# The second mixer's entry in another order, latents in three weight pieces, keys without zeros, and the pooling in full f32

## The reference

```python
diff = pooled - xg                      # mean of the last 2, 4, 8 or 16 rows, less x
y = jnp.einsum('bsgc,gcd->bsgd', diff, w_grp)   # 4 groups, 256 x 256
x = layer_norm(ALPHA * x + y * scale, ...)
```

```python
mod = c_act @ w_ada[l] + b_ada[l]
sh_a, sc_a, g_a, sh_f, sc_f, g_f = jnp.split(mod[:, None, :], N_MOD, axis=-1)
h = rms_norm(x, g_mix[l]) * (1.0 + sc_a) + sh_a
x = x + g_a * hybrid_mixer(h, ...)      # differential attention and latent attention
...
proj = h @ w_in                         # dq, dk, dv, q_lat (384), kv_lat (256), k_rope (64)
q = rms_norm(q_lat, g_q_lat) @ w_q_up
kv = rms_norm(kv_lat, g_kv_lat) @ w_kv_up
```

## Time and profile before

| | us |
|---|---|
| median of 3 executions | 1013.44 (1012.06 to 1014.56) |
| profiled execution | 1015.39 |
| its span in the trace | 1013.6 |
| mean granted clock of TensorE, share of full speed | 0.989 |
| TensorE busy | 980.2 |
| VectorE busy | 657.5 |
| ScalarE busy | 496.5 |
| GpSimd busy | 62.0 |

### The profile page before, as it was taken

The page is one execution under the profiler, slowest core; times in us unless marked ns, Lnnn a source line. Parts: engine busy times, 40 slices in busy tenths (PEclk is TensorE's granted clock), DMA queues, the critical chain, the costliest instruction groups (busy, mean ns, idle before and its releaser), DMA issues.

```text
span 1013.6 us, 14978 instructions
## 1 busy us (share of the span) xinstructions
PE 980.2 (97%) x6249; PEld 891.3 (88%) x6249; DVE 657.5 (65%) x759; ACT 496.5 (49%) x662; POOL 62.0 (6%) x98
## 2 busy tenths in 40 slices
PE   6999999999999999889999999999999899999996
PEld 6888888989999999788899999988998699999996
DVE  4885468658777655875796766448778674545453
ACT  4657363535654555245275545425765464343431
POOL 1000131001000002100100000002200000000000
PEclk9999999999999999999999999998999999999998
DMA  8864355636988876363298898543553247565611
GB/s 271 282 210 161 129 172 178 232 105 208 342 283 288 268 273 213 119 211 121 85 331 312 273 307 273 196 145 123 177 191 108 90 137 231 182 188 187 185 65 42
DMA packets 114527, 200.03 MB, mean 197 GB/s; under 512 B 5122, under 2 KB 85368, under 8 KB 111388
## 3 DMA queue, kind: packets, MB, share of 16 engines
q1 hardware_dynamic: 111340, 188.38, 55.8%
q0 software_dynamic: 2832, 10.16, 2.9%
q10 hardware_dynamic: 288, 0.52, 0.1%
HBM read 198.00 MB, written 1.05 MB: 196 GB/s over the span
## 4 chain that ended last, share of the span: by engine, by line
PE 82%; DVE 8%; ACT 3%; issue 2%; SPq 1%; POOL 1%; DMA 1%; DVEq 0%; POOLq 0%; ACTq 0%
PE WB L336 11%; PE WB L332 11%; PE WB L329 11%; PE YB L348 10%; PE YB L357 10%; PE YB L353 10%; PE YB L393 4%; PE WB L348 2%; PE WB L353 2%; PE WB L357 2%; ACT wh L1015 2%; DVE U L1787 2%; DVE wl L1558 2%; PE WB L655 1%; PE WB L636 1%
## 5 line engine op out<-in xcount | busy, mean ns | idle before, releaser
L1558 DVE TENSOR_TENSOR wl<-raw,wh 128x2048 fp32r<-128x2048 f32 (+2 forms) x153 | 347.9, 2281 | 190.5 <-ACT wh L1015 189.9
L1015 ACT CAST wh<-raw 128x2048 fp32r<-128x2048 f32 (+2 forms) x153 | 288.8, 1892 | 46.3 <-PE YB L357 24.7
L329 PE MATMUL WB<-XH,wh 128*128 128x256 f32 x1024 | 145.9, 285 | 0.0
L332 PE MATMUL WB<-XH,wl 128*128 128x256 f32 x1024 | 144.3, 284 | 0.0
L336 PE MATMUL WB<-XL,wh 128*128 128x256 f32 x1024 | 143.7, 283 | 0.0
L329 PEld LDWEIGHTS WB<-XH,wh 128*128 128x128 f32 x1024 | 135.1, 192 | 3.3 <-issue 0.3
L332 PEld LDWEIGHTS WB<-XH,wl 128*128 128x128 f32 x1024 | 132.7, 193 | 0.0
L336 PEld LDWEIGHTS WB<-XL,wh 128*128 128x128 f32 x1024 | 132.1, 192 | 0.0
L348 PE MATMUL YB<-wh,FHT 128*128 128x512 f32 x360 | 112.5, 394 | 0.0
L353 PE MATMUL YB<-wl,FHT 128*128 128x512 f32 x360 | 111.6, 391 | 0.0
L357 PE MATMUL YB<-wh,FLT 128*128 128x512 f32 x360 | 111.4, 391 | 0.0
(11 more groups left out here) (316 smaller groups left out, 1115.9 us busy)
## 6 DMA issues: line engine op xcount, KB each, us to landing
raw<-in_mlp_w SPq DMA_DIRECT2D x64, 1024.0 KB, 6.2
raw<-in_w_ada SPq DMA_DIRECT2D x24, 1024.0 KB, 5.1
raw<-in_mlstm_w_in SPq DMA_DIRECT2D x12, 1024.0 KB, 7.5
raw<-in_w_ffn_gate SPq DMA_DIRECT2D x11, 1024.0 KB, 5.3
raw<-in_w_ffn_up SPq DMA_DIRECT2D x11, 1024.0 KB, 5.5
raw<-in_w_ffn_down SPq DMA_DIRECT2D x11, 1024.0 KB, 5.0
raw<-in_mem_w_kv SPq DMA_DIRECT2D x8, 1024.0 KB, 5.2
raw<-in_xattn_wq SPq DMA_DIRECT2D x8, 1024.0 KB, 7.1
```

Source lines behind the costliest of these rows:

```text
L329: e.matmul(o, H[:, at(k)], xh[:, k, :], start=k == 0, stop=False)
L332: e.matmul(o, L[:, at(k)], xh[:, k, :], start=False, stop=False)
L1015: f = e.copy(w[:, 0:a * b], raw[:, 0:a * b])
L1558: f = e.tensor_tensor(L[:, 0:a * b], raw[:, 0:a * b], H[:, 0:a * b].bitcast(F32), ALU.subtract)
```

## The change

- **Pooling.** Its chunk is no longer converted. ScalarE copies the difference in f32 to `S`, TensorE multiplies it in full f32 with the scaled `raw` buffer, two products of 256 columns a group; `pool_lows` is gone, and norm 10's `scale` waits for the window products that read x. The buffer is free for its next load (the fourth query chunk of layer 1) when the last pooling product is done. All later chunks move up one slot.
- **Norms.** `Norm.first` does centre, centre, scale, scale.
- **Modulation.** All 32 products go into the second MLP, 8 behind each of `up(14)`, `down([12])`, `up(15)`, `down([13])`; one copy and two small steps put them out, behind the conversions.
- **Entry.** The latent weights are three chunks (1920, 1792, 1920 columns), the second by two DMAs. Gate rows on TensorE: the transpositions of t = 0 stand behind two of the four instead of three. VectorE scales t = 0 ahead of the last head of norm 12, and forms the low parts between the centring and scaling of t = 1. ScalarE squares first, converts the last latent chunk, and copies gate rows between norm quarters and squares. Latents go out in the order kl 0, ql 0, kl 1, ql 1 on all engines, with kl in the banks that ql had, and their squares go to a place of their own.
- **Keys.** `KD` and `KPE` stand once; a score product takes 64 of the partitions of both operands. The memsets and their wait are gone, and one copy takes the place of two.
- **Tables.** SyncE issues them ahead of the same chunk as before, behind the last gate row instead of the second modulation.

```diff
-    for kh in range(2):
-        add(("kl", kh), rows(w2i, 4 * kh, 4, 1920, 2240), 4, 320)
-    for kh in range(2):
-        add(("ql", kh), rows(w2i, 4 * kh, 4, 1536, 1920), 4, 384)
+    add(("lat", 0), rows(w2i, 0, 6, 1920, 2240), 6, 320)
+    add(("lat", 1), [rows(w2i, 6, 2, 1920, 2240), rows(w2i, 0, 3, 1536, 1920)], 1, 2 * 320 + 3 * 384)
+    add(("lat", 2), rows(w2i, 3, 5, 1536, 1920), 5, 384)
...
-        KD = AR[:, 1024:3072].rearrange("p (h s c) -> p h s c", h=4, s=2)
+        KD = AR[:, 1024:2048].rearrange("p (h c) -> p h c", h=4)
...
-        mms = [n for n, c in enumerate(chunks) if c[0][0] != "ada"]
+        mms = [n for n, c in enumerate(chunks) if c[0][0] not in ("ada", "pool")]
...
                 for j in range(3, 16):
                     up(j)
+                    if also and j > 13:
+                        also(2 * j - 28)
                     down([j - 2])
-                if late:
-                    late()
+                    if also and j > 13:
+                        also(2 * j - 27)
                 down([14, 15])
...
-                    p = tm(m, 2, 256, 512 * g, 512 * g + 256, YB[2 * t + g // 2][:, 256 * (g % 2):256 * (g % 2) + 256],
-                           t, 2 * g, True, True, hi=lambda k: e.wait_ge(*act_pool[t, g]),
-                           lo=lambda k: e.wait_ge(*dve_pool[t, g]))
+                    e.wait_ge(*act_pool[t, g])
+                    for k in range(2):
+                        p = e.matmul(YB[2 * t + g // 2][:, 256 * (g % 2):256 * (g % 2) + 256],
+                                     S[:, 2 * g + k, 128 * t:128 * t + 128],
+                                     P[:, 512 * g + 256 * k:512 * g + 256 * k + 256], start=k == 0, stop=k == 1)
...
-                    if n == h == 1:
+                    if n == 1 and h == 0:
                         ln_turn("mix", 0, 0)
                         ln_turn("mix", 0, 1)
...
-            e.wait_ge(*act_mod["g", 0, 0])
-            modulation(1, YB[0])
...
-                    e.matmul(W[:, 0:128], DQ[:, h, 0:128], KD[:, h, m, 0:128], start=True, stop=True)
+                    ps = slice(64 * m, 64 * m + 64)
+                    e.matmul(W[:, 0:128], DQ[ps, h, 0:128], KD[ps, h, 0:128], start=True, stop=True)
...
-                    for h in range(2):
-                        self.centre(0, h)
-                        self.scale(0, h)
+                    self.centre(0, 0)
+                    self.centre(0, 1)
+                    self.scale(0, 0)
+                    self.scale(0, 1)
...
             n12.head(1, 0)
-            n12.head(1, 1)
             rms_z("mix", 0, 0)
             rms_z("mix", 0, 1)
-            n12.centre(1, 0)
-            n12.scale(1, 0)
+            n12.head(1, 1)
             evac("mix", 0, 1, g, b)
             rms_low("mix", 0, 0)
             rms_low("mix", 0, 1)
+            n12.centre(1, 0)
+            rms_low("mix", 0, 2)
+            n12.scale(1, 0)
+            rms_low("mix", 0, 3)
             n12.centre(1, 1)
             n12.scale(1, 1)
-            modulation_out(1, YB[0])
-            rms_low("mix", 0, 2)
-            rms_low("mix", 0, 3)
-            lo_to(M["w2", 1, 15] + 4)
+            lo_to(M["lat", 2])
...
-            step(e.memset(KD[64:128, :, 0, :], 0.0))
-            step(e.memset(KD[0:64, :, 1, :], 0.0))
...
-                    e.wait_ge(*(w_ada[n - NR] if before[0] == "ada" else w_lo[M[before]]))
+                    e.wait_ge(*(w_ada[n - NR] if before[0] == "ada" else
+                                pe_rows["pool", 1, 1] if before[0] == "pool" else w_lo[M[before]]))
```

More of the change, by code:

```diff
@@ L254, in build_program @@
         CS = AR[:, 8192:8704].rearrange("p (n c) -> p n c", n=2)
+        JL = [KV[:, 384 * n:384 * n + 384] for n in range(4)]
         QN = KV[:, 0:1024].rearrange("p (h c) -> p h c", h=4)
@@ L281, in build_program @@
         s_raw = [sem(f"raw_in{i}") for i in range(NR)]
-        landed = lambda n: (s_raw[n % NR], 16 * (n // NR + 1))
+        parts = lambda n: chunks[n][1] if isinstance(chunks[n][1], list) else [chunks[n][1]]
+        landed = lambda n: (s_raw[n % NR], 16 * sum(len(parts(i)) for i in range(n % NR, n + 1, NR)))
         ends, freed, bank_of, bv_of = {}, {}, {}, {}
@@ L1149, in scalar, with norm @@
             hi_to(M["wout", 2] + 3)
-            def norm(s, g, b, between):
+            def norm(s, g, b, between, amid=None):
                 for t in range(2):
@@ L1452, in mixed @@
                 hi_to(M["wout2", (0, 2, 1, 3)[n]] + 3)
[L1454 to L1457 removed]
+            for t in range(2):
+                hi_to(M["lat", 2] + 1 + t)
+                latent("kl", t, KL[:, t, :], 256)
+                latent("ql", t, QL[:, t, :], 384)
             steps = {"k": dqk, "n": minus_lambda, "l": latents, "z": rope_key, "v": dv, "u": kv_up, "q": q_up,
@@ L2141, in mixed @@
                 lo_to(M["wout2", (0, 2, 1, 3)[n]] + 3)
-            for name, dst, n in (("kl", KL, 256), ("ql", QL, 384)):
-                lo_to(M[name, 1] + 3)
-                for t in range(2):
-                    latent(name, t, dst[:, t, :], n)
+            for t in range(2):
+                lo_to(M["lat", 2] + 1 + t)
+                latent("kl", t, KL[:, t, :], 256)
+                latent("ql", t, QL[:, t, :], 384)
             steps = {"k": dqk, "n": minus_lambda, "l": latents, "y": rotary, "v": dv, "u": kv_up, "q": q_up,
@@ L2293, in gpsimd @@
                 rms_stats("mix", (t,))
-            e.wait_ge(*po_ln["r", "mix", 1])
-            step(e.memset(KD[64:128, :, 0, :], 0.0))
-            step(e.memset(KD[0:64, :, 1, :], 0.0))
-            step(e.memset(KPE[64:128, 0, :], 0.0))
-            e.memset(KPE[0:64, 1, :], 0.0).then_inc(po_mix.add("zero"))
-            e.wait_ge(*po_mix["zero"])
-            for name, n in (("kl", 256), ("ql", 384)):
-                for t in range(2):
+            for t in range(2):
+                for name, n in (("kl", 256), ("ql", 384)):
                     w = cols((name, t), 2)
```

195 lines of the change are left out of this document (93 added, 102 removed).

## The result

The changed kernel takes 1004.46 us in the median of four executions (1002.79 to 1005.49), the kernel before, run beside it, 1014.0: a ratio of 0.9903, with a 95% interval of 0.9885 to 0.992. That is faster by 1%, well outside the 0.3% that can be told from no change. The profiled execution took 1004.83 us with a span of 1003.0, against 1015.39 and 1013.6 before; the forecast was 1004.9 for the profiled execution and 1003.0 for the median.

The account below looks back on a forecast made before the run. TensorE, busy 97% of the span, was taken as the bound. Terms 7.6 + 0.8 - 2.1 + 4.7 + 1.1 = 12.1 us, less 1.6 for one clock fall, gave 10.5: 1004.9 profiled, 1003 median, range 998.5 to 1008.5.

Parts of the forecast that it names:

- Pooling, 7.6 us: Pooling through norm 10: second half's products begin at 434.5 instead of 442.17, gaining 7.6 us (bounds 5 to 9).
- Centring twice 425.0: VectorE in norm 10: after the variance at 423.6, both centrings end at 425.0, so the transposition starts at 425.75.
- A load behind a wait: SyncE's fourth query chunk load waits for the pooling weights' buffer; it lands near 434, costed at nothing.
- Order in the norms, 0.8 us: Norms 00, 01, 11: TensorE's 1.0 us of waits at L393 go, 0.13 us twice returns; 0.8 us gained (0 to 1.2).
- Modulation, -2.1 us: Second MLP: four bursts add 3.67 us, the old burst's 1.6 us clock loss goes; -2.1 us, or -8.5 if each falls.
- the rival in which the clock falls behind every burst: Modulation bursts and entry: the clock falls behind each burst and at the entry; gain 3.5 us, 1010; chance 0.09.
- Entry, 4.7 us: Second mixer's entry: first product of the next weights at 709.9 instead of 714.8; 4.7 us gained (1.5 to 8).
- after the 2 us wait at the turn: One of two places named for the one unplaced clock fall, 1.6 us, taken off the sum; the other was behind a burst.
- Keys without zeros, 1.1 us: Mixer keys: the waits at L435 (0.6) and L877 (0.7) go, score products take the same time; 1.1 us (0 to 1.4).
- No fall: Rival for the whole kernel: no fall of the clock, the full 12.1 us gained, 1001.3; chance 0.20.
- The entry gives nothing: Rival at the mixer's entry: TensorE, early, waits for weights or halves instead; gain 5.8 us, 1007.6; chance 0.12.
- Slower: Rival: each of four bursts loses 3.3 us to the clock; -1.1 us, 1014.5, or 1016.8 with the entry's; chance 0.03.

Follow-up runs that it names:

- the vector early: The changed kernel with norm 10's gain vector loaded early into another tile, ahead of norm 02's second-half steps; 1001.65 us in its one profiled execution.
- the pooling alone: The kernel before with only the pooling part of the change; 1008.53 us (median of 7) against 1013.49, ratio 0.9965.
- the copies back: The changed kernel with keys and rotary keys copied by two copies of 64 partitions instead of one of 128; 1002.85 us in its profiled execution.

## Why the prediction was right, point by point

The forecast of 10.5 us and the measured 10.6 are closer than the terms are. For pooling, norms, modulation, entry (with the fall of 1.6 us taken off) and keys the forecast had 7.6, 0.8, -2.1, 3.1 and 1.1 us, and 6.67, 1.55, -2.06, 3.74 and 0.66 were measured. The misses of -0.9, +0.75, +0.6 and -0.4 us cancel. That the gain is about 10 us was worked out; that the sum is right to 0.1 us is luck.

- **Pooling, 7.6 us.** The second half's products begin at 434.49, where 434.5 was forecast. But 1.01 us of that is an earlier start, which the sum counted once more under the norms. The pooling itself gave 6.67 us: 4.79 alone (28.08 to 23.29), 1.88 by the order. Two errors met at 434.5: up to norm 10's variance (forecast for 423.6, ended at 422.5) the trace runs about 1 us ahead of the walk, and there VectorE lost 1.10 us to the load. "Centring twice 425.0" assumed the gain vector in place, and the load of 3.9 us behind norm 02's last scaling was late. I had followed SyncE's queue with care ("A load behind a wait", which did cost nothing) and left out GpSimd's. With the vector early the stretch is 20.12 us, where the walk, started at 413.9, had 20.6 (the earlier trace rows have 414.09, so 20.4). The clock stayed at 1.00 from the pooling to the second half's products in every kernel with the new pooling, as the walk assumed; before, it was 0.85 over 11.1 us. So a part of the 4.79 us is a fall that did not come, some 1.5 us if it costs what it does elsewhere here; no run took this apart.
- **Order in the norms, 0.8 us.** Mis-sized: 1.01 in the norms before the pooling and 0.54 in norm 11, so 1.55 where 0.8 stood; with norms 10 and 12 it is 4.4, most of which the forecast had inside its walks of the pooling and the entry. The term counted only TensorE's idle time at L393; where the other half us was lost no run took apart.
- **Modulation, -2.1 us.** It cost 2.06 (244.17 to 246.23, with the norms in their old order); the rest of the -1.52 is norm 11. No burst of 1.84 us was followed by a fall, in ten profiles with four bursts each, so the rival in which the clock falls behind every burst is out for them. Bursts of 3.63 us had a fall in some cases.
- **Entry, 4.7 us.** 3.74 with a fall behind the wait, 5.27 without (23.20). The forecast had 4.7 without and took one fall of 1.6 off the whole. A fall there costs 1.5 (24.73 less 23.20). The stretch at 0.50 of the kernel before, 2.25 us in the forecast, was worth 2.00: the pooling alone has the old entry without a fall and takes 26.47. The place, "after the 2 us wait at the turn", was one of the two named. TensorE's wait was 1.96 us against 2.0; the start of the key latent was a microsecond better than the walk. GpSimd's step ends 0.17 us behind VectorE's conversion, so the value with the lock was the right one to take. The Trainium skill's rule (SBUF — State Buffer, "SBUF: two separate sides") would have it so, and the trace agrees: 1.38 us for a step of 0.30.

  The entry and the modulation belong together, since one sent its short products to the other. From the second half's products to the first key weight it is 272.64 us before and 270.42 after, so 2.2 us less. By the prices above, an estimate, 2.0 of them are the clock's (1.5 behind the old burst and 2.0 at the old entry, less 1.5 at the new one), and the order in the norms gives 0.54 and 0.84. Nothing is left for all other edits of the entry together, although one of them, the memsets that are gone, is worth 1.14 alone. TensorE starts the latents 6 us earlier and then waits 1.96 us for the second half. What the three weight pieces and the new orders on ScalarE and VectorE are worth, each for itself, no run shows.
- **Keys without zeros, 1.1 us.** The two waits are worth 1.15, where 1.1 was forecast. But the step "half the rows but the same columns, so the same time" failed both ways. The scores of the differential attention became faster, 1.31 to 0.86 us a head:

```profile
782.52 0.38 PE L877 MATMUL WB<-AR 128*128 128x128 f32 x2
...
783.82 0.49 PE L885 MATMUL WB<-IDN,U 128*128 128x128 f32 x3
```
```profile
771.78 0.50 PE L887 MATMUL WB<-AR 64*128 64x128 f32 x4
...
772.64 0.55 PE L895 MATMUL WB<-IDN,U 128*128 128x128 f32 x3
```

  (before, then after), the rotary ones slower, 1.31 to about 2.0. Four heads of each give 4 x 0.45 - 4 x 0.7, so 1.0 us is lost and next to nothing would be left of 1.15; that it is 0.66 is put down here to a shorter wait for VectorE later, at L895 (1.76 us, before 2.34). This is a sum over the timeline and not the result of a run: halving the changes of height did not shorten the mixer.
- **The median.** Forecast from the profiled execution less 1.95, measured 0.4 below it: that is the 1.5 us between 1003.0 and 1004.46. The offset was taken from a profiled execution in which the mean clock was 0.989; it isn't a constant of the kernel.
- **The rivals.** "No fall" came about at the entry and in the mixer of one kernel only, the copies back, which is the same up to the entry; the changed kernel itself had two falls in both profiles. "The entry gives nothing" is wrong for the entry's own stretch, 3.74 us, and near the truth for entry and modulation without the clock's share. "Slower" had nothing for it.

## What to carry to other kernels

When work is taken from an engine, follow every load whose buffer that engine's old place kept out of sight, on each queue that issues one: the pooling lost 1.3 of 8 us to a vector whose load stood in GpSimd's queue. Compare two profiles stretch by stretch and with the granted clock beside it; a whole-kernel time here moved by some 1.5 us for each fall that came or stayed away in dense work, as much as the edits under test, and by nothing for one that lay ahead of a wait for another engine. And put short products into full work in small bursts: four of 1.84 us cost their own time, one of 7.3 cost 6.4 us more.

## What the runs showed of the hardware

- **The clock falls or not behind the same wait.** Behind 1.96 us of idle at the entry it fell for 3 to 3.5 us in the changed kernel and stayed up in the kernel with the copies back. In the mixer, around waits of 1.65 and 1.76 us, it fell in 11 profiles and not in 3. Executions of the changed kernel took 1002.79 and 1003.22 us at a mean clock of 0.996, 1004.08 to 1005.49 at 0.994 and 1006.01 at 0.993; the pooling alone ran from 1006.01 at 0.996 to 1013.95 at 0.987. What decides it no run here shows.
- **A fall of the clock ahead of a wait for another engine cost nothing here.** In three profiles it came 71.3 to 72.3 us behind the first key and query weight, ahead of the wait for VectorE: the mixer took 98.74 to 98.79 us, and 98.71 without a fall. In seven with the changed mixer it came 77.1 to 77.8 us behind, where the wait ends: 100.03 to 100.38.
- **A change of height costs TensorE some 0.18 us.** Two heads of rotary scores: 2.63 us at one height, 3.41 with four changes, 4.09 with eight, so 0.20 and 0.17 us a change. The Trainium skill (TensorEngine Tiling (Array Packing), "Key Properties") says that a change of the tiling mode drains TensorE; the trace agrees, and this rule spoke against a part of the change and was not weighed in the prediction.
- **Products of 64 partitions that follow each other, on one half of the partitions and then on the other, take less than two of 128.** 0.86 us for four where 1.31 was. The Trainium skill (TensorE: Matmul & The Clock Gate, "Part 3: Packing small matmuls — row/col tiling") says that small products on different tiles of the array can run at the same time, which would explain it; no run here took it apart from other causes.
